# Four copies per quarter made by ScalarE from one load, and a final norm twelve half quads later

## The reference

```
h  = modulate(rmsnorm(x, norm1_g), shift1, scale1)
... stick-breaking attention, sliding-window attention, gates ...
x  = x + gate1 * (merged @ w_out)
h2 = modulate(rmsnorm(x, norm2_g), shift2, scale2)
x  = x + gate2 * peer_ffn(h2, ...)
out = rmsnorm(x, final_g)
```

```
act = gelu(einsum('td,thkd->thk', xb, expert_u[experts]))
w   = softmax(best_s) * act
out = einsum('thk,thkd->td', w, expert_v[experts])
```

## Time and profile before

| | |
|---|---|
| median of 3 runs | 3476.81 us (3470.8 to 3479.14) |
| the profiled execution's own time | 3469.32 us |
| its span, first to last instruction | 3467.5 us |
| busy: PE, DVE, ACT, POOL | 65%, 62%, 32%, 34% |
| moved by DMA | 1265.20 MB, mean 365 GB/s |
| of these the gathers (software queue) | 1074.03 MB |
| mean granted clock of PE | 0.789 |

### The profile page before, as it was taken

How to read it: one execution, slowest core, us unless ns; L and a number is a source line. 1 busy time by engine, 2 the same in 40 slices (tenths; PEclk the granted TensorE clock), 3 DMA queues, 4 the chain that set the end, 5 groups by cost and what they waited for, 6 DMA issues and landing times.

```text
span 3467.5 us, 40799 instructions
## 1 busy us (share of the span) xinstructions
PE 2267.1 (65%) x13784; PEld 1206.2 (35%) x13784; DVE 2137.3 (62%) x4890; ACT 1113.6 (32%) x3069; POOL 1166.7 (34%) x1033
## 2 busy tenths in 40 slices
PE   7788659996997765888787878577433333333333
PEld 5646534453553433333344444234211111111111
DVE  1111576657556787776777665678766566656654
ACT  2210136544331223666653332222211121122111
POOL 0000123433332323443344433333344444444443
PEclk9889779997998887888897989789666556565565
DMA  6263769999999999999999999999899999999997
GB/s 246 82 249 122 247 259 405 368 380 357 363 396 386 384 367 366 421 420 393 401 415 414 400 387 417 412 418 358 318 421 421 403 405 421 421 396 408 421 421 307
DMA packets 206838, 1265.20 MB, mean 365 GB/s; under 512 B 24779, under 2 KB 30955, under 8 KB 75556
## 3 DMA queue, kind: packets, MB, share of 16 engines
q0 software_dynamic: 147616, 1074.03, 76.5%
q1 hardware_dynamic: 59012, 188.57, 14.8%
HBM read 1247.28 MB, written 15.22 MB: 364 GB/s over the span
## 4 chain that ended last, share of the span: by engine, by line
DMA 26%; DVE 10%; PE 9%; issue 3%; ACT 2%; POOL 0%; DVEq 0%; POOLq 0%; ACTq 0%
DMA ring<-in_uv,idx 26%; PE pb L902 5%; DVE ring L1529 5%; ACT wts L1161 1%; PE pb L755 1%; DVE acc L1536 0%; DVE kidx L1442 0%; PE pb L828 0%; DVE zone L1444 0%; DVE kidx L1448 0%; DVE vals L1446 0%; ACT gl L1158 0%; PE pb L848 0%; DVE vals L1440 0%; ACT zone L1052 0%
## 5 line engine op out<-in xcount | busy, mean ns | idle before, releaser
L617 POOL DMA_INDIRECT ring<-in_uv,idx x1024 | 1163.6, 1136 | 2268.1 <-PE pb L902 1674.6
L1529 DVE CUSTOM_DVE_ANT_0 ring<-h2r,ring 128x1024 f32<-128x1024 f32 x1024 | 1233.9, 1223 | 634.2 <-DMA ring<-in_uv,idx 628.7
L902 PE MATMUL pb<-ring,wts 128*32 128x256 f32 x8192 | 745.9, 526 | 959.3 <-ACT wts L1161 959.2
L902 PEld LDWEIGHTS pb<-ring,wts 128*32 128x32 f32 x8192 | 306.6, 143 | 1370.7 <-ACT wts L1161 1109.8
L1158 ACT ACTIVATE gl<-dots 128x4 f32<-128x4 f32 x256 | 52.5, 205 | 1332.3 <-DVE dots L1529 1331.5
L944 ACT ACT_TABLE_LOAD x223 | 286.1, 1283 | 4.7 <-PEq L1676 0.7
L1161 ACT ACTIVATE wts<-gm,gl 128x32 f32<-128x32 f32 x1024 | 245.1, 310 | 8.5
L882 PE MATMUL pb<-zone,wst 128*128 128x384 f32 (+1 forms) x768 | 245.8, 476 | 1.7 <-issue 1.7
L882 PEld LDWEIGHTS pb<-zone,wst 128*128 128x128 f32 x768 | 151.8, 203 | 89.2 <-issue 23.9
L828 PE MATMUL pb<-hT,wst 128*128 128x384 f32 x512 | 175.2, 499 | 0.7 <-ACT ys L1075 0.7
L1282 DVE SCALAR_TENSOR_TENSOR zone<-pb,zone 128x384 f32<-128x384 f32 (+2 forms) x120 | 57.0, 476 | 165.1 <-ACT zone L998 163.6
(11 more groups left out here) (173 smaller groups left out, 2617.6 us busy)
## 6 DMA issues: line engine op xcount, KB each, us to landing
wst<-in_w_all SPq DMA_DIRECT2D x148, 512.0 KB, 8.5
ring<-in_w_all SPq DMA_DIRECT2D x50, 512.0 KB, 11.1
ring<-in_w_ada SPq DMA_DIRECT2D x48, 512.0 KB, 7.8
h2r<-h_scratch SPq DMA_DIRECT2D x128, 128.0 KB, 7.9
ring<-in_uv,idx POOLq DMA_INDIRECT x1024, 14.8
ys<-mod_scratch SPq DMA_DIRECT2D x9, 512.0 KB, 16.6
zone<-in_x SPq DMA_DIRECT2D x8, 512.0 KB, 4.5
hT<-in_x SPq DMA_DIRECT2D x8, 512.0 KB, 13.3
```

What stands on the lines that cost most here:

```text
L617: pool.indirect_dma_start(ring[:, n % RING, :], None, uv, bass.IndirectOffsetOnAxis(ap=idx4[:, piece % 2, col:col + 1], axis=0)).then_inc( ...
L902: m = pe.matmul(pb[32 * f:32 * f + 32, 6 + q // 2, (q % 2) * 256:(q % 2 + 1) * 256], wts[:, n % WBUFS, :], ring[:, n % RING, D + 256 * f:D ...
L1529: dve.tensor_tensor_reduce(u, h2r[:, q, :], u, 1.0, 0.0, ALU.mult, ALU.add, dots[:, n % 16:n % 16 + 1]).then_inc(dots_done, 1)
```

## The change

For blocks 1 to 7 the 128 rows of h2 are loaded once, into `x1b`, which is free between the Square of one block's norm and the load of the next residual. ACT makes the sixteen copies (four per quarter) from there into `h2r`, 32 partitions by 1024 each, at half quads 58, 60, 62 and, for the last quarter, at 0 of the next block. Block 0 keeps its 16 DMAs. The buffer's new use moves other steps: the residual of block b is loaded at hq 4 of block b+1, after the copies, its final norm stands at hq 16 to 18 in place of 2 to 4 and its store at hq 20; the load of h2 is at hq 44. For the last block the residual is loaded at hq 44 of that block and the norm stays at the end.

```diff
+        in_rows_h2, copied = sem("in_rows_h2"), sem("copied")
...
-                def copies(b, q):
-                    need(sp, dots_done, b * PER_BLOCK - (QUARTERS - 1 - q) * TILES)
+                def first_copies(q):
+                    need(sp, h2_out[0], 16)
+                    for j in range(TILES):
+                        sp.dma_start(h2r[32 * j:32 * j + 32, q, :], h2_dram[32 * q:32 * q + 32, :]).then_inc(in_h2r[q], 16)
+                def rows_h2(b):
+                    need(sp, f_square, b - 1)
                     i, g = place_of(b)
                     need(sp, h2_out[i], 16 * uses_of(i, g))
-                    for j in range(TILES):
-                        sp.dma_start(h2r[32 * j:32 * j + 32, q, :], h2_dram[b * P + 32 * q:b * P + 32 * q + 32, :]).then_inc(in_h2r[q], 16)
+                    sp.dma_start(x1b[:], h2_dram[b * P:(b + 1) * P, :]).then_inc(in_rows_h2, 16)
                 def residual(b):
                     need(sp, f_square, b)
+                    need(sp, copied, QUARTERS * min(b + 1, NB - 1))
                     need(sp, x1_out, 16 * GROUPS[place_of(b)[1]][1])
...
                             if hq == 4 and blk:
+                                residual(blk - 1)
+                            if hq == 20 and blk:
                                 store(blk - 1)
-                            if hq == 12:
-                                residual(blk)
-                            if hq in (58, 60, 62) and blk + 1 < NB:
-                                copies(blk + 1, (hq - 58) // 2)
+                            if hq == 44:
+                                if blk + 1 < NB:
+                                    rows_h2(blk + 1)
+                                else:
+                                    residual(blk)
...
-                        if blk + 1 < NB:
-                            copies(blk + 1, 3)
...
+                def copies(b, q):
+                    act.wait_ge(in_rows_h2, 16 * b)
+                    act.wait_ge(dots_done, b * PER_BLOCK - (QUARTERS - 1 - q) * TILES)
+                    for j in range(TILES):
+                        op = act.activation(h2r[32 * j:32 * j + 32, q, :], x1b[32 * q:32 * q + 32, :], ACT.Copy)
+                    op.then_inc(copied, 1)
...
-                        if hq == 2 and blk:
+                        if hq in (58, 60, 62) and blk + 1 < NB:
+                            copies(blk + 1, (hq - 58) // 2)
+                        if hq == 0 and blk:
+                            copies(blk, 3)
+                        if hq == 16 and blk:
                             final(blk - 1, 0)
-                        if hq == 3 and blk:
+                        if hq == 17 and blk:
                             final(blk - 1, 1)
...
-                    if h == 0 and i == 0:
-                        dve.wait_ge(in_h2r[q], 64 * (b + 1))
+                    if h == 0 and i == 0 and b == 0:
+                        dve.wait_ge(in_h2r[q], 64)
+                    elif h == 0 and i == 0:
+                        dve.wait_ge(copied, QUARTERS * (b - 1) + q + 1)
...
-                        if hq in (2, 3, 4) and blk:
-                            final(blk - 1, hq - 2)
+                        if hq in (16, 17, 18) and blk:
+                            final(blk - 1, hq - 16)
```

More of the change, by code:

```diff
@@ L577, in _ @@
                 for q in range(QUARTERS):
-                    copies(0, q)
+                    first_copies(q)
                 background = spans(rest, *(mixer(g) for g in range(1, NG)))
```

## The result

The changed kernel takes 3429.36 us (median of 4, 3428.42 to 3432.64) against 3474.11 for the kernel before in the same comparison: ratio 0.9868, 95% interval 0.9853 to 0.9884. That is 1.3% or 44.7 us faster, where 42.8 us were forecast. The two profiled executions differ by less, by 36.7 us (3469.32 and 3432.64), as the one lies low and the other high among its kernel's runs; where the other 8 us lie, no trace shows.

A forecast was written before the change was run, and what follows sets the result against it. Late block ends were taken as bound by DMA gathers, others by DVE or ACT. Gains of 21.8 (blocks 5, 6), 8, 3, 3 and 7 (norm) sum to 42.8 us: 3476.8 - 42.8 = 3434, range 3405 to 3459.

The forecast's parts named there:

- the likeliest case: Whole kernel: the main forecast, 3434 us for the median, chance 0.62, its own range 3411 to 3458.
- Copies at the ends of blocks 5 and 6: Ends where gathers are waited for: removed DMAs worth 12.2 us, less 1.25 for the added load, net 10.9 each.
- 3 to 4: End of block 3: 8 us gained of 10.9, since TensorE is busy 46 of 61 us; bounds 0 and 10.9.
- 2 to 3: End of block 2: 3 us gained, ACT having 47.6 us of work in 52; bounds -12 and 10.9.
- 0 to 1: End of block 0: 3 us gained, DMA waits of 8.0 against ACT copies delaying TensorE; bounds -16 and 8.0.
- The norm: Starts of blocks 2 and 5: moving the final norm out of DVE's unbroken run gains 3.5 us each, 7 together.
- Ends 1 to 2 and 4 to 5: Ends of blocks 1 and 4, where DVE sets the pace: removing the copies gains 0.
- SP's waits: SP waits at half quads 4 and 20 in place of 58 to 63: costed at nothing, either way.
- ACT takes the DMA's place: Rival: at five ends ACT's 16 us of copies delay TensorE, 80 against 59.6 gained; 20 slower, 3497 us; chance 0.07.
- The slow quads are not the copies' doing: Rival: only the bytes go, 3.7 us at four ends, plus 7 for the norm: 22 us, 3455; chance 0.09.

The follow-up runs named there:

- runs 5 to 8: Kernel before, h2r DMAs altered: one 128-partition DMA per quarter, 3439.02 us; other source rows, 3476.37; sixteen 128-partition DMAs, 3444.54; other partition order, 3478.68.
- Run 4: The changed kernel with every ACT copy into h2r made twice: 3458.5 us, ratio 0.9958 to the kernel before.
- run 1: The kernel before with only the final norm, its store and the next residual moved later, the 16 DMAs kept: 3472.67 us, ratio 0.999.
- run 2: The changed kernel with the final norm put back early, at half quads 4 to 6: 3429.06 us, ratio 0.9869 to the kernel before.
- run 5: The kernel before with one 512 KB DMA to 128 partitions per quarter in place of four to 32, blocks 1 to 7: 3439.02 us, ratio 0.9891.
- run 10: The changed kernel with ACT's copies behind the background slots of their half quad, not ahead of them: 3439.32 us, ratio 0.9895 to the kernel before.
- run 11: The changed kernel with DVE making two of each quarter's four copies at the ends of blocks 0 and 2: 3424.41 us, ratio 0.9848 to the kernel before.

## Why the prediction was right

The forecast was 3434 us, the measurement 3429.4, inside the likeliest case's own range of 3411 to 3458. By its terms:

- *Copies at the ends of blocks 5 and 6*, 10.9 each. Four intervals fell by 12.1 and 12.0; with the added load block 6 gained 10.7, and block 5 15.1 less the norm's 2.7, so 12.4. Right. That the excess over the bytes (7 us) is due to the narrow transfers was argued then and is shown now, by runs 5 to 8. In block 5 the extra 1.5 fits the residual's load moving to where DMA stood idle, which was not tested.
- *3 to 4*, 8 of at most 10.9: block 3 gained 12.5. Under-sized. I had cut the 10.9 for TensorE's 46 busy us of 61; the stretch got shorter all the same, with TensorE at 55 us of 62 in the window after (which holds 292 of its matmuls, where the one before held 240). Why it gained 1.6 more than the term's upper bound is open.
- *2 to 3*, 3: block 2 gained 1.9, of which 2.3 is the norm, so nothing was left. The step was right in kind, ACT being the new bound, and its size wrong: I had counted 12 us of copies into the stretch, and it was 17 (4 x 4.25), since the last quarter's copies fall into the fourth interval too.
- *0 to 1*, 3: block 0 is 0.9 us longer, within its scatter. Its four intervals are 4.1 shorter. Run 4 shows that ACT is close to the bound there as well (10.7 us for 17 of copies).
- *The norm*, 7: the first quads of blocks 2 and 5 fell from 26.0 and 25.8 us to 23.7, as foretold, but run 1 gives 3 for the whole kernel (blocks 2 and 5 gain 5.0, block 3 gives 2.3 back), and run 2, with the norm early again, nothing. By run 1 over-sized more than twice over. Part of it comes back where the norm now stands, with the store's bytes: block 5's tenth quad takes 12.4 in place of 9.9 us in run 1 and in the changed kernel. DVE's wait of 8.4 us for the norm's root in block 1 is gone (1.2 us are left in the whole kernel), and block 1 is no shorter for it.
- *Ends 1 to 2 and 4 to 5*: copies nothing, and nothing it was: 54.2 to 54.1 and 53.9 to 53.9.
- *SP's waits* at nothing: run 5 keeps them as they were, and its 44.9 us at the ends of blocks 5 and 6 are block 7's 39.7 and the bytes' 5.0, which leaves 0.2 for them there. Elsewhere they were not isolated.
- *Two slips* in its working enter no term: the drain and the copies leave 1.5 us of a quad by its own numbers, not 1.6, and the 112 copies at its estimate of 0.95 us are 106 us, not 107.

That the sum came within 2 us is in part luck. Between the two profiled executions 36.8 us were gained and not 42.8: the ends of blocks 3, 5 and 6 gave 6 more than their terms, and the ends of blocks 0 and 2, the norm and the drift of the others some 12 less.

Of the rivals, "ACT takes the DMA's place" is real at the end of block 2, but costs there what the DMAs had cost. It had to hold at all five mixed ends to decide, and at those of blocks 1, 3 and 4 ACT was idle enough. "The slow quads are not the copies' doing" fell with run 1: with the DMAs kept the four intervals stay at 51.9 and 52.9 us, without them they are 39.8.

## What to carry to other kernels

Find two stretches of one trace that do the same work with and without the suspect: the ends of blocks 5 and 7 priced a DMA pattern at 12 us where its bytes alone said 5. Moving work from a full resource to one that is idle on average pays only where it is idle at that place; ask for each stretch what stands in the receiver's queue. Behind an instruction that waits for another engine new work starts late (run 10); ahead of it, it can use that wait. Where the receiver is short of time at one place only, the work there can be split between two engines: run 11 took the end of block 2 from 50.0 to 43.1 us.

## What the runs showed of the hardware that was not expected

Beside a saturated stream of gathers, 128 KB transfers to 32 partitions bring the total down from 421 to about 290 GB/s while they last; as 128 partitions by 1 KB the same size does not (four intervals of 45.1 against 52 us). The order in which the partition groups are served made no difference. Which side of such a transfer is slow, its 32 partitions or its 32 rows, is open. And DVE makes the same 32x1024 float32 copy in 0.69 us that takes ACT 1.05. Its row in run 11, and ACT's in the changed kernel (ns min/median/max):

```profile
L1561 DVE COPY h2r<-x1b x16: 683/686/691, 813.4 to 1656.9; 32x1024 f32<-32x1024 f32 x16
```

```profile
L1176 ACT ACTIVATE h2r<-x1b x112: 1038/1054/1057, 808.6 to 3093.7; 32x1024 f32<-32x1024 f32 x112
```
